# Two-layer attention and PEER encoder: order of work at the start of the first layer

## The reference, cut to what matters

```python
for l in range(DEPTH):                       # DEPTH = 2
    h = rms_norm(x, norm_mix[l]) @ w_in[l]   # 1024 -> 2400 columns
    h_a, h_b, h_c, h_d = split(h)            # four attention mixers
    ...                                      # o_a, o_b, o_c, o_d
    x = x + heads.reshape(B, S, D_MIX) @ w_out[l]
    x = x + peer_ffn(rms_norm(x, norm_ffn[l]), ...)   # 128^2 single-neuron experts
```

## Time and profile before

| | us |
|---|---|
| median of 3 runs | 1622.99 |
| lowest, highest | 1621.75, 1624.92 |
| profiled execution, its own time | 1623.32 |
| its span, first to last instruction | 1621.5 |

### The profile page before, as it was taken

How to read it: one execution, slowest core, us unless ns; L and a number is a source line. 1 busy time by engine, 2 the same in 40 slices (tenths; PEclk the granted TensorE clock), 3 DMA queues, 4 the chain that set the end, 5 groups by cost and what they waited for, 6 DMA issues and landing times.

```text
span 1621.5 us, 31846 instructions
## 1 busy us (share of the span) xinstructions
PE 1589.9 (98%) x11548; PEld 1548.6 (96%) x11548; DVE 1065.9 (66%) x2517; ACT 544.5 (34%) x1424; POOL 698.2 (43%) x556
## 2 busy tenths in 40 slices
PE   7999999999999999999999999999999999999998
PEld 6888999999999998999978889999999999999998
DVE  4783789688886653444357847996888866544443
ACT  5675521655554000000067754226555530000000
POOL 6615614455553433343165266045535535333431
PEclk9999999999999999999999999999999999999999
DMA  9026279899999999999881252889999999999996
GB/s 359 7 100 260 92 283 338 313 409 409 409 410 387 368 409 409 410 409 410 337 290 52 98 216 92 314 332 337 410 410 409 409 360 392 410 409 410 409 410 274
DMA packets 141942, 525.77 MB, mean 324 GB/s; under 512 B 16160, under 2 KB 19744, under 8 KB 139424
## 3 DMA queue, kind: packets, MB, share of 16 engines
q1 hardware_dynamic: 86336, 322.57, 51.1%
q0 software_dynamic: 55520, 202.14, 31.8%
HBM read 523.60 MB, written 1.05 MB: 324 GB/s over the span
## 4 chain that ended last, share of the span: by engine, by line
PE 89%; DMA 4%; DVE 3%; ACT 2%; issue 1%; POOL 1%; SPq 0%; DVEq 0%; ACTq 0%; POOLq 0%
PE ps L618 87%; DMA ring<-in_peer_v 2%; PE ps L615 2%; DMA nat<-in_peer_v 1%; ACT grid L298 0%; DVE grid L1401 0%; DVE negmax L1405 0%; DMA x<-in_x 0%; DVE grid L1454 0%; ACT grid L970 0%; DVE x L1459 0%; ACT grid L1069 0%; ACT wh L1006 0%; POOL wl L587 0%; ACT grid L956 0%
## 5 line engine op out<-in xcount | busy, mean ns | idle before, releaser
L618 PE MATMUL ps<-grid,ring 128*128 128x160 f32 (+1 forms) x3712 | 523.3, 299 | 3.2 <-DMA ring<-in_peer_v 2.1
L618 PE MATMUL ps<-grid,nat 128*128 128x160 f32 (+1 forms) x3712 | 522.6, 299 | 2.1 <-DMA nat<-in_peer_v 1.2
L618 PEld LDWEIGHTS ps<-grid,ring 128*128 128x128 f32 x3712 | 508.7, 190 | 6.5 <-issue 6.3
L618 PEld LDWEIGHTS ps<-grid,nat 128*128 128x128 f32 x3712 | 508.7, 190 | 4.4 <-issue 4.4
L1683 DVE SCALAR_TENSOR_TENSOR grid<-grid,amount 128x1024 f32<-128x1024 f32 x96 | 123.3, 1285 | 151.0 <-DMA grid<-in_peer_v,lists 150.2
L600 POOL DMA_INDIRECT gath_a<-in_u_rows,lists x96 | 131.0, 1365 | 178.8 <-DVE dots L1652 124.0
L1683 DVE SCALAR_TENSOR_TENSOR grid<-gath_a,amount,grid 128x1024 f32<-128x1024 f32 x94 | 120.8, 1285 | 130.3 <-DMA gath_a<-in_peer_v,lists 128.9
L600 POOL DMA_INDIRECT gath_a<-in_peer_v,lists x96 | 112.9, 1176 | 205.6 <-PE ps L618 131.5
L580 POOL TENSOR_TENSOR wl<-grid,wh 128x512 fp32r<-128x512 f32 (+2 forms) x128 | 143.3, 1144 | 119.9 <-ACT wh L1006 98.3
L600 POOL DMA_INDIRECT grid<-in_peer_v,lists x96 | 108.4, 1129 | 175.2 <-PE ps L618 113.4
L1006 ACT ACTIVATE wh<-grid 128x512 fp32r<-128x512 f32 (+2 forms) x128 | 68.1, 575 | 321.6 <-PE ps L618 321.4
(11 more groups left out here) (198 smaller groups left out, 1767.4 us busy)
## 6 DMA issues: line engine op xcount, KB each, us to landing
nat<-in_peer_v SPq DMA_DIRECT2D x128, 512.0 KB, 13.6
ring<-in_peer_v SPq DMA_DIRECT2D x128, 512.0 KB, 13.5
nat<-in_peer_u SPq DMA_DIRECT2D x104, 512.0 KB, 7.4
ring<-in_peer_u SPq DMA_DIRECT2D x104, 512.0 KB, 7.2
grid<-in_peer_u SPq DMA_DIRECT2D x48, 512.0 KB, 6.0
grid<-in_peer_wq SPq DMA_DIRECT2D x8, 2048.0 KB, 10.0
grid<-in_w_out SPq DMA_DIRECT2D x2, 4096.0 KB, 13.3
grid<-in_w_in SPq DMA_DIRECT2D x3, 2048.0 KB, 16.6
```

The source lines that it names most:

```text
L618: return nc.tensor.matmul(dst, a, b, start=first, stop=last)
```

## The change

In layer 0 alone:

- ScalarE begins with a Copy of one column of `ones`, so that the table load in front of it comes at once. The copy waits for VectorE's memset of `ones` (a new semaphore, `ones_set`).
- ScalarE then alternates high parts of x and roundings: high part 0, high part 1, piece 0, high part 2, piece 1, high part 3, pieces 2 and 3, and then the other four high parts.
- PE turns x's first half, then the identity six times into bank 3, then makes the products of pieces 0 to 3, then turns x's second half, then makes the products of pieces 4 to 7.

Layer 1 keeps its order, and no DMA is moved.

```diff
-WARM_HEADS, WARM_X, WARM_MIX = 28, 28, 5
+WARM_HEADS, WARM_X, WARM_MIX, WARM_START = 28, 28, 5, 6
...
-                    for half in range(2):
+                    def turn_new_x(half):
+
                         for tt in range(NT):
...
+                    turn_new_x(0)
+                    if l:
+                        turn_new_x(1)
...
-                    project(0)
+                    if l == 0:
+                        keep_busy(3, WARM_START)
+                        project(0, 0, KD // 2)
+                        turn_new_x(1)
+                        project(0, KD // 2)
+                    else:
+                        project(0)
                     project(1)
...
                     if l == 0:
-                        high_input(0, 0, KD // 2)
-                    high_pieces(0, 2)
-                    if l:
+                        act.wait_ge(ones_set, 1)
+                        A(lamt[:, 6:7], ones[:, :], ACT.Copy)
+                        high_input(0, 0, 1)
+                        for n in range(1, KD // 2):
+                            high_input(0, n, n + 1)
+                            high_pieces(n - 1, n)
+                        high_pieces(KD // 2 - 1, KD // 2)
+                        high_input(0, KD // 2)
+                    else:
+                        high_pieces(0, 2)
                         turn_y(past[y_chunk] - 3)
-                    high_pieces(2, 4)
-                    high_input(0, KD // 2 if l == 0 else 0)
+                        high_pieces(2, 4)
+                        high_input(0)
                     high_pieces(4, KD)
...
-                        v.memset(ones[:, :], 1.0)
+                        v.memset(ones[:, :], 1.0).then_inc(ones_set, 1)
```

More of the change, by code:

```diff
@@ L318, in build @@
          lists_ready, best_shift, wexp_ready, lists_t, listt_ready, hots_ready, dist_ready, hota_act, gate_done, gated,
-         y_done, y_chunk, lam_ready, gain_in, picked, gath_used, acts_ready, yt_act, yt_dve, yt_cleared, y_turned, mean_ready, root_ready, rs0_ready, heads0_ready) = (S(n) for n in (
+         y_done, y_chunk, ones_set, lam_ready, gain_in, picked, gath_used, acts_ready, yt_act, yt_dve, yt_cleared, y_turned, mean_ready, root_ready, rs0_ready, heads0_ready) = (S(n) for n in (
             "xsq_done xn_ready xt_done w_high w_rest w_used h_ready hsq_ready sq_used gqm_ready hn_ready rs_used kr_ready "
@@ L326, in build @@
             "lists_ready best_shift wexp_ready lists_t listt_ready hots_ready dist_ready hota_act gate_done gated "
-            "y_done y_chunk lam_ready gain_in picked gath_used acts_ready yt_act yt_dve yt_cleared y_turned mean_ready root_ready rs0_ready heads0_ready").split())
+            "y_done y_chunk ones_set lam_ready gain_in picked gath_used acts_ready yt_act yt_dve yt_cleared y_turned mean_ready root_ready rs0_ready heads0_ready").split())
         PER_LAYER = {}
```

## The result

The changed kernel takes 1625.7 us (median of 22 runs, 1623.57 to 1628.28) against 1623.33 (22 runs, 1621.47 to 1624.92). The ratio is 1.0015 with a 95% interval of 1.0009 to 1.0022: 2.4 us slower, just short of the 0.2% that I had called the line. The three intervals overlap between 1.0014 and 1.0022, so the change costs 2.3 to 3.6 us, and on which side of 0.2% it lies can't be told.

The account below looks back on a forecast made before the run. PE, busy 98% of the span, was taken as the bound, handing on any loss at the start; 0 (table) + 0 (idle turns) + 3.0 + 0.4 = +3.4 us gave 1626.4 us against 1622.99, range 1623.6 to 1628.3.

Parts of the forecast that it names:

- The mark and the chain: Layer 0's start: piece 7's rounding on ScalarE, at 17.22, marks the stage; all behind it keeps its distance.
- The table load at 0: ScalarE's start: the earlier load brings 0, since the first activation still waits for the gains, landing at 7.35.
- Six idle turns at 0, both ways: PE behind the first half's turns, from about 6.0 to 7.3: they cost nothing, as PE waits there anyway.
- The alternation, 0.16 won by bounds of the landing: ScalarE: piece 0's rounding waits for the first weights, so starts at 9.18 instead of 9.34, 0.16 us won.
- The four products ahead of the turns, +3.0: PE turns x's second half only from 16.29; piece 7's rounding moves from 17.22 to 20.22, +3.0 us.
- the rise moves before and after alike, by half of it each: Clock rise up to 1.5 us off 15.2 shifts both kernels alike, by half of it each.
- The clock's fall behind the gap, +0.4: PE's new 2.4 us gap likely halves the clock for 3.3 us, costing 1.65 less 1.2 of slack: +0.4 us.
- The sum, +3.4, and 1626.4: Whole kernel: all terms together +3.4 us, giving 1626.4 against 1622.99, 0.21% more; main case's chance 0.62.
- (a): Rival: six idle turns keep the clock high when the four products start; +0.8 us, 1623.8; chance 0.12.
- (b): Rival: the clock rises only after the four products, past 17.2; +5.0 us, 1628.0; chance 0.16.
- (c): Rival: a later wait takes up most of the loss; +0 to +1 us, about 1623.5; chance 0.06.
- (d): Rival: the change gains because x's second half lands late; 1619.5 beside 1623.0; chance 0.04.

Follow-up runs that it names:

- e1: The kernel before with ScalarE's table load and tiny copy at the start, nothing else: 1621.86 us, ratio 0.9997 to the kernel before.
- e3: The changed kernel with ScalarE's old order, which also took the early table load away: 1626.55 us, ratio 1.0026 to the kernel before.
- e7: The kernel before with 16 idle turns on PE between x's first and second half: 1621.71 us, ratio 0.9998 to the kernel before.
- e4: The changed kernel without its six idle turns: 1625.19 us, ratio 1.0020 to the kernel before.
- e2: The kernel before with ScalarE's new alternation of high parts and roundings alone: 1622.52 us, ratio 1.0002 to the kernel before.
- e12: The changed kernel itself, measured a third time, beside versions that fill PE's gaps: 1625.72 us, ratio 1.0022 to the kernel before.
- e8: The changed kernel itself, measured again beside other experiments on one chip: 1626.13 us, ratio 1.0024 to the kernel before.
- e6: The changed kernel with 22 idle turns on PE behind the turns of x's second half: 1626.42 us, ratio 1.0030 to the kernel before.
- e5: The changed kernel with 18 idle turns instead of 6 ahead of the products: 1622.43 us, ratio 1.0009 to the kernel before.
- e11: The kernel before with 16 idle turns on PE between x's halves, run a second time: 1621.60 us, ratio 0.9997 to the kernel before.
- e10: The changed kernel with 18 idle turns ahead of the products and 22 behind the second half's turns: 1622.71 us, ratio 1.0004 to the kernel before.

## Why the prediction was right, and where not

**The mark and the chain** held. I had taken the rounding of piece 7 and the squares behind it for the end of the stage. The squares moved by 2.35, 3.1 and 3.4 in the three profiles of the changed kernel, the first eviction by 2.7, 3.5 and 3.4, and the total by 2.4 to 3.9 in the three comparisons.

**The table load at 0**: right, by e1. Its cover is thinner than the 0.25 us of the earlier trace rows looked: in e3 and e7 x's first half was turned later, the load ended at 7.69 and 7.63, and the high part began at once.

**Six idle turns at 0, both ways**: nothing against it in e4, one profile and an interval that is as wide as 3 us.

**The alternation, 0.16 won by bounds of the landing**: the first rounding came at 9.32, 0.02 earlier, since the weights landed at 9.29 instead of 9.12; e2 has no difference. Right.

**The four products ahead of the turns, +3.0**: the mechanism was right in each link. From the fifth high part to the fifth rounding I had 1.85 us, and the trace has 1.85 (16.58 to 18.43). The gap of PE was 2.35, where I had 2.4. What was off is the term that says when the four products are over: 15.68 instead of 16.29, because the clock rose near 13.5 and not at 15.2, the moment that I took over from the kernel before. The first product came later (9.96 instead of 9.75), its first matmul on a rest stood at 10.89 instead of 10.74, and the step from that one to the next took 0.46 us, not 0.293; so the product of piece 0 was over at 12.23 instead of 11.91, which took back part. In e12, with the rise near 15.8, the same step measured +3.4 (squares at 21.01 against 17.63), in e8 +3.1. So +3.0 lay in the midst of what was measured, though the moment of the rise that it rests on was not the changed kernel's. I had written that the rise moves before and after alike, by half of it each. That holds for one moment of rise in both kernels, but two single profiles draw two moments: 2.35, 3.1 and 3.4 are such draws.

**The clock's fall behind the gap, +0.4**: in the profile of the changed kernel 0.34 (2.69 at piece 12 against 2.35 at the squares), 0.3 against e6. Each of the four falls lasted 3.4 us, where I had 3.3. The size was right where it happens; it happens in four of six profiles, and no comparison of times resolves it.

**The sum, +3.4, and 1626.4**: measured 1625.7 at first, with 2.4, and then 3.9 and 3.6 in the two comparisons beside the experiments. The outcome that I gave the higher chance, slower by more than 0.2%, was not the first comparison's, and the three together lie on the line.

**The rivals.** (a) came with 18 turns and not with six (e5); nothing between was run. (b), a rise behind the four products, was never seen; the latest was near 15.8, with the four over at 16.7 (e12). (c), 0 to 1 us at the end, falls by the three comparisons of the total, whose intervals begin at 1.5, 2.3 and 2.1 us. (d) needs a late second half of x; the old order's turns of it began between 9.77 and 10.22 in every profile.

## What to carry to other kernels

Work that is pulled ahead of a short step is only free if nothing behind that short step is a chain: here eight turns of 0.1 to 0.2 us released a chain of 1.85 us on two other engines, and the products that used to hide the chain were the ones moved ahead of it. Ask of each early start what used to run beside the step that it pushes back. And before an order is changed to win a microsecond at the start, look at the pitch of the matmuls there: the low clock cost the old order 1.6 to 2 us there, and 16 to 18 idle turns ahead of the products took it back in the trace, where six that ended 2.3 us ahead showed no effect. In the totals that gain wasn't shown (e7, e11).

## What the hardware showed that I had not expected

- The moment of the clock's rise differs from profile to profile by 2.5 us in like programs (13.3 to 15.8), and behind one and the same idle gap of 2.35 us the granted clock fell in four profiles of six, 1.2 to 2.1 us after PE had begun to work again. The Trainium skill (TensorE: Matmul & The Clock Gate, What's actually happening) calls the low level the default, says that the moment isn't tied to the kernel's start, and has it vary by 0.5 us either way. The traces agree but for the size; a single profile's moment is a draw, and I had used it as a constant.
- Idle turns needn't reach quite up to the products: in e10 the 18 turns ended 1.17 us ahead of the first product, and it ran at the high level all the same.
- The granted-clock column reads 1.00 ahead of the first change that it records, though the pitch of 0.293 us for 352 columns shows 1.2 GHz.
- Behind a wait the first matmul of 352 columns takes longer from start to start: 0.43 us at 9.96 in the changed kernel, and 0.46 at 10.89 behind the wait for GpSimd's rest, against 0.293 for those that follow at the low level. The first one right behind the turns did so too in the kernel before (0.44 at 11.39).
- The table load of 1.28 us is followed by its first activation within 0.02 us (0.75 to 2.05 in the changed kernel, 6.41 to 7.70 in e3); the drain that the Trainium skill adds (ScalarE: Activation LUTs, What ACT_TABLE_LOAD costs) doesn't show at either place.
